# A spread order of the steps of a two-way recurrence, with products of ones where a step has no results or no modulation rows

## The reference

```python
def wkv_scan(state0, r, decay, kk, b, v, k, reverse):
    def step(S, inp):
        r_t, w_t, kk_t, b_t, v_t, k_t = inp
        sa = jnp.einsum("bhvk,bhk->bhv", S, kk_t)
        S = (S * w_t[:, :, None, :] - sa[..., None] * b_t[:, :, None, :]
             + v_t[..., None] * k_t[:, :, None, :])
        return S, jnp.einsum("bhvk,bhk->bhv", S, r_t)
...
        mod = jax.nn.silu(c) @ ada_w[l] + ada_b[l]
        sh1, sc1, g1, sh2, sc2, g2 = [m[:, None, :] for m in jnp.split(mod, 6, axis=-1)]
```

## Time and profile before

| | |
|---|---|
| median of 3 runs | 1587.11 us (1568.42 to 1589.66) |
| the profiled execution | 1576.66 us, span 1575.1 us |
| PE busy | 1493.3 us, 95% |
| DVE busy | 918.2 us, 58% |
| ACT busy | 598.1 us, 38% |
| mean granted clock of TensorE | 0.960 |
| mean DMA rate | 88 GB/s |

### The profile page before, as it was taken

One profiled execution on the slowest core, in us unless ns is written; L12 is line 12 of the kernel. 1 busy time (PEld: TensorE's weight loads), 2 busy tenths in 40 slices (PEclk: granted clock), 3 DMA queues, 4 the chain that ended last, 5 costly groups with the idle time before them and its releaser, 6 DMA issues.

```text
span 1575.1 us, 35522 instructions
## 1 busy us (share of the span) xinstructions
PE 1493.3 (95%) x14858; PEld 1232.4 (78%) x14858; DVE 918.2 (58%) x1499; ACT 598.1 (38%) x1037; POOL 271.8 (17%) x290
## 2 busy tenths in 40 slices
PE   5999989999999998999999998998999999999997
PEld 3788865788889777887877886877878888888885
DVE  4424245676668738888886224767565655555232
ACT  4422345333343534443443223536664322232221
POOL 0000024554443010111111121000021111111110
PEclk9999999778689999999999998999999999999998
DMA  9232201222220222232323222221112232232221
GB/s 370 97 110 79 81 0 56 76 91 84 83 63 4 83 81 80 80 107 80 107 82 108 92 92 81 88 81 55 54 54 82 106 107 85 101 107 92 92 92 72
DMA packets 38987, 139.15 MB, mean 88 GB/s; under 512 B 3152, under 2 KB 3664, under 8 KB 38480
## 3 DMA queue, kind: packets, MB, share of 16 engines
q1 hardware_dynamic: 38720, 135.24, 25.2%
q10 hardware_dynamic: 144, 2.10, 0.3%
HBM read 135.22 MB, written 2.10 MB: 87 GB/s over the span
## 4 chain that ended last, share of the span: by engine, by line
PE 80%; DVE 13%; ACT 3%; issue 3%; DMA 1%; ACTq 0%; DVEq 0%; SPq 0%
PE bank L716 56%; PE bank L898 9%; DVE ffn_sb L3153 5%; PE bank L725 3%; PE bank L662 2%; PE bank L992 1%; DVE w_up L2581 1%; PE bank L1064 1%; PE bank L1004 1%; PE bank L1554 1%; PE bank L929 1%; DMA arena<-w 1%; PE bank L655 1%; ACT w_up L1675 1%; ACT arena L2171 1%
## 5 line engine op out<-in xcount | busy, mean ns | idle before, releaser
L716 PE MATMUL bank<-hf_hi,w_up 128*128 128x512 f32 x1376 | 424.2, 389 | 0.0
L716 PEld LDWEIGHTS bank<-hf_hi,w_up 128*128 128x128 f32 x1376 | 258.4, 188 | 53.2
L716 PE MATMUL bank<-hf_lo,w_up 128*128 128x512 f32 x688 | 269.2, 391 | 4.5 <-DVE w_up L2581 4.5
L716 PE MATMUL bank<-act_hi,w_down 128*128 128x512 f32 x704 | 216.9, 389 | 0.0
L898 PEld LDWEIGHTS bank<-arena 64*64 64x64 f32 x4224 | 160.7, 154 | 35.7 <-issue 25.2
L898 PE MATMUL bank<-arena 64*64 64x32 f32 (+1 forms) x4224 | 172.3, 237 | 10.1 <-issue 6.1
L1675 ACT ACTIVATE w_up<-ring 128x1024 fp32r<-128x1024 f32 x87 | 91.9, 1058 | 215.7 <-PE bank L716 215.7
L2581 DVE TENSOR_TENSOR w_up<-ring,w_up 128x1024 fp32r<-128x1024 f32 x87 | 106.9, 1229 | 96.9 <-ACT w_up L1675 96.9
L716 PEld LDWEIGHTS bank<-hf_lo,w_up 128*128 128x128 f32 x688 | 129.2, 188 | 35.9 <-DVE w_up L2581 8.9
L3153 DVE SCALAR_TENSOR_TENSOR ffn_sb<-ffn_sb 128x512 f32<-128x512 f32 x176 | 151.5, 861 | 5.4
L716 PEld LDWEIGHTS bank<-act_hi,w_down 128*128 128x128 f32 x704 | 132.2, 188 | 27.4
(11 more groups left out here) (350 smaller groups left out, 2399.7 us busy)
## 6 DMA issues: line engine op xcount, KB each, us to landing
ring<-w SPq DMA_DIRECT2D x76, 1024.0 KB, 4.9
ring<-w SPq DMA_DIRECT2D x32, 704.0 KB, 4.0
ring<-w SPq DMA_DIRECT2D x64, 256.0 KB, 3.7
arena<-w SPq DMA_DIRECT2D x8, 1024.0 KB, 18.7
x<-xT SPq DMA_DIRECT2D x1, 2048.0 KB, 9.9
x<-xT ACTq DMA_DIRECT2D x1, 2048.0 KB, 8.4
outT<-x SPq DMA_DIRECT2D x4, 512.0 KB, 2.7
arena<-ctxT SPq DMA_DIRECT2D x1, 1024.0 KB, 18.9
```

Source lines behind the costliest of these rows:

```text
L716: ins = mm(out, w[:, a, k, :], of_block(b, k0 + k), start=first and k == 0 and m == 0, stop=last and k == n - 1 and m == 2)
```

## The change

The lists of PE, ACT and DVE are written in another order. On PE, in the second loop, both `state_terms` stand together behind level 3, `results` before and after nx of level 4, `turned` in level 5, the two `ada_part` in levels 5 and 6, and `scores` of the next chunk earlier. `ada_select(n)` and `mod_out(n)` of that loop move into the next step (as n - 1), and the wait of `scores` for `mod` is loosened by one for direction 1 where q > NCC. A new function `awake` issues one product of a 128x128 matrix of ones with itself, read four times over (512 columns), into bank[d][0], which nobody reads. It is called twice in a step without results (n = 2, 3) and twice in a step without modulation rows (n >= 7), 12 times in all. The matrix `warm` is made by one copy on ACT, and `rstd_c` is declared wider.

```diff
-        rstd_c = sb("rstd_c", [P, TC])
+        rstd_c = sb("rstd_c", [P, P])
+        warm = sb("warm", [P, P], F32R)[:, :]
...
                 if q > 0:
-                    pe.wait_ge(s[("ada_row", "mod")[d]], 8 + min(before, 8))
+                    rows = before - d if q > NCC else before
+                    pe.wait_ge(s[("ada_row", "mod")[d]], 8 + min(rows, 8))
...
+            warm_x = warm.unsqueeze(1).broadcast_to([P, 4, P])
+
+            def awake(n, d):
+
+                pe.wait_ge(s["low_tanh"], 2)
+                done("nk", d, 2 * min(n + 3, NC))
+                pe.wait_ge(s[("ada_row", "mod")[d]], 8 + min(n + 1, 8))
+                done("y_out", d, n - NCC + 1)
+                mm(bank[d][0][:, :], warm, warm_x, start=True, stop=True)
...
             for n in range(NCC - 2, NC - 1):
                 m, q = n + 1, n + 2
                 nx(m, 0, 2)
+                nx(m, 1, 2)
+                scores(q, 1)
                 updates(n, 0)
-                nx(m, 1, 2)
+                dx(m, 1, 2)
+                dx(m, 0, 2)
                 scores(q, 0)
...
                 results(n, 0)
+                if n < NCC:
+                    awake(n, 0)
                 nx(m, 0, 4)
...
+                ada_part(n, 0)
+                if n >= 7:
+                    awake(n, 0)
                 nx(m, 0, 6)
-                ada_select(n)
                 nx(m, 1, 6)
+                ada_part(n, 1)
+                if n >= 7:
+                    awake(n, 0)
                 dx(m, 0, 6)
                 dx(m, 1, 6)
...
             act_f(table_at, ones[:, 0:1], ACT.Exp)
+            act_f(warm, ones, ACT.Copy).then_inc(s["low_tanh"], 1)
```

192 lines of the change are left out of this document (96 added, 96 removed).

## The result

The changed kernel is slower, not faster: a median of 1604.86 us (4 runs, 1584.66 to 1605.89) against 1588.38 us (4 runs, 1568.42 to 1593.57), ratio 1.0161, 95% interval [1.0094, 1.0227]. The profiled execution took 1604.62 us, its span is 1602.9 us at a mean clock of 0.948 (before 1576.66, 1575.1 and 0.960). Ten later runs of the same kernel have a median of 1590.27 us and a ratio of 1.0086 [1.0024, 1.0149]; all 14 have a mean of 1594.6 us, against 1584.8 us over the 91 runs of the kernel before in this study. So the cost is about **10 us, 0.6%**, and the first four runs overstate it. Single runs of the kernel before lie between 1558.2 and 1607.5 us. The ratios leave out runs more than 1.5% above the fastest of their kernel, which here drops ordinary runs as well, so I give the mean of all runs with its standard error beside each ratio.

A forecast was written before the change was run, and what follows sets the result against it. PE's time was taken as the bound, with 87 us of the recurrence at half clock. 24.2 - 2.7 - 1.0 = 20.5 us gained from 1576.7 gives 1556, raised slightly to 1557 us; range 1538 to 1582.

The forecast's parts named there:

- What bounds the kernel: Whole kernel: PE's time counts nearly everywhere, TensorE busy 95%; in the recurrence 87 us run at half clock.
- what half clock costs: Recurrence steps: each microsecond at half clock costs 0.41 us, with 0.35 and 0.47 as ends.
- Step 1: PE's order in the second loop: heavy products spread among level groups cut half clock from 87 to 28 us, gaining 24.2 us.
- Step 4: Second loop: ada_select and mod_out one step later, DVE and ACT lists following PE's order; costed at nothing, DVE waits left to rivals.
- Rival D: Recurrence steps: PE's waits for DVE take the clock's place, 1 to 1.5 us a step; 1566 to 1575 us, chance 0.07.
- the prediction's own sign: Steps n = 4 to 6 in the later profile: clock 1.00 yet still over 23 us would mean Rival D.
- The rule that the prediction named: TensorE's clock is lost through PE's idle gaps between bursts of matmuls; the forecast held that step n = 8 disagrees.
- E: Recurrence up to n = 6: once lost, the clock does not come back, adding 65 us; 1642 us, chance 0.04.
- Step 2: Twelve products of ones in n = 2, 3 and 7 to 10: 0.222 us each, 2.7 us lost.
- Step 3: state_terms(n, 1) close behind updates(n, 1), waiting for ACT's copy: 1 us lost over nine steps, between 0 and 7.
- The base: Starting time: profiled run of 1576.7 us, median 10.4 us above it, difference supposed mostly half clock that the change takes away.

The follow-up runs named there:

- h4_masks_in_level5: The kernel before with only DVE's masks of the next scores (first_level) moved from level 4 to level 5; mean 1602.9 us, ratio 1.0142.
- h1_masks_and_turned: The changed kernel without the products of ones, with DVE's masks back in level 4 and PE's turned back in levels 3 and 4; mean 1604.5 us, ratio 1.014.
- i1_after_fill_ahead: The changed kernel with ten products of ones added in the step n = -1, behind its turned(m, 0); mean 1592.5 us.
- e8_after_again: The changed kernel run again with no edit; mean 1592.4 us, ratio 1.0086.
- e4_before_again: The kernel before run again with no edit; mean 1583.9 us, ratio 0.9893 against itself.

## Why the prediction was wrong

**What bounds the kernel, and what half clock costs: right.** Over the runs of each kernel the time grows by 0.35 to 0.48 us for each microsecond at half clock (0.45 over the 91 runs of the kernel before, 0.44 over all); 0.41 was taken.

**Step 1, the order on PE: this is the term that failed. 24.2 us of clock were forecast; over the whole kernel it gave none (139 us at half clock against 137).** What it said of n = 0 to 6 was right in kind and under half in size. Over the four profiles with the whole changed order these steps hold 47 us at half clock on average (41, 52, 37, 57), against 71 over five with the order before (86, 57, 83, 69, 62). The forecast took the 86 of one profile as the kernel's own and 28 for what remains. The gain is 24 x 0.43 = 10.3 us. Its direct cost was put at nothing, and there most goes back: PE stands 18.1 us instead of 13.2 in these steps, the four ones of n = 2, 3 cost about 1, and some 3 us are not accounted for. The steps together are 172.6 against 174.0 us, **1.4 us** gained, which profiles that spread over 9 and 13 us cannot tell from nothing. That n = 8 would keep its clock was wrong; it lost it in every profile of the changed order.

**Step 4, the DVE list "follows PE's order" and costs nothing: this is why step 1's gain did not stay.** It moved `first_level` beside POOL's burst and ahead of x_out. n = 7 and 8 take 48.8 us on average against 37.6, 11.2 us lost, of which (22 - 2) x 0.43 = 8.6 are clock and the rest ones and waits. In each of the eight steps n = 7 and 8 of these four profiles PE waits some 0.6 us for x_out and the clock falls less than 3 us later. Moving these two lines alone did the same in the kernel before. Putting them back alone did not cure the changed order, so there they are a cause and not shown to be the only one. 11.2 lost less 1.4 gained is 9.8 us, and the means of all runs differ by 1594.6 - 1584.8 = 9.8 too; that they meet is luck. The errors are 2 to 3 us on the means and more on the steps, and the sum leaves out what stands behind n = 8: from the start of n = 9 to the end the four profiles take 1084.6 us on average and the five 1081.4, with a fall of the clock for 10.2 us in n = 10 in three of the four, and for 3.4 us in two of the five. The account at equal clock is firmer: of the 8.9 us, some 3 are the ones, and PE stands 5.8 us longer from n = 0 to 8 (19.4 against 13.6).

**Rival D had the engine and not the price.** It said that DVE in line would take the clock's place at 1 to 1.5 us a step, as plain waits that only shrink the gain. The waits are small (0.6 us), but in n = 7 and 8 the clock fell behind each of them, and at 0.44 the 3.4 to 10.2 us at half clock that follow cost 1.5 to 4.5 us; and they fell on steps that had nothing to gain, which no rival looked at. By the prediction's own sign, n = 4 at full clock and 26.0 us speaks for D. Two readings behind D's low chance were off: PE waited for DVE's x_out too (1.2 us on L2769, beside the 1.6 on L2760), and DVE is busy 78% and not 81% in n = 8. The rule that the prediction named from the Trainium skill ("TensorE: Matmul & The Clock Gate", "HAM oscillation — how this bites in real kernels"), that the clock is lost through gaps, deserved more weight than I gave it by n = 8 alone: with PE's list untouched, small gaps ahead of a level run did decide. It is not the whole of it either: at the end of n = 6 the clock falls without a wait over 0.2 us in the first profile of before (449.5 us). E, the slower rival, was another mechanism and did not occur: the clock comes back in every step.

**Step 2, the ones:** forecast 2.7; 3.0 by their spacing, 2.0 in the changed order and 5.6 in the old one at equal clock. **Step 3, state_terms close behind updates:** no wait of PE for the update's copy appeared in its profiles, so its 1 us was nothing.

**The base.** The forecast was made against a profiled run of 1576.7 us and took the 10 us up to the median for more of the same half clock within the steps. Most of it was the stretch ahead of n = 0, which comes and goes without the change: filling it gave 10 us. The forecast and its range, 1538 to 1582, would have had to stand on the median, 1587; moved up by 10 us the range still ends below the 1594.6 of all 14 runs.

Left open: what sets off the "issue" stops beside the transfers, and why there is somewhat more of them; why one wait before a level run costs the clock and another does not; and a changed order whose masks keep clear of POOL in all steps, which was not found.

## What to carry to other kernels

Where TensorE's clock hangs on small products, look at every wait ahead of a run of them, also those of half a microsecond, and also in the steps that run well now: a list that is rewritten for all steps can lose there what it gains elsewhere. A moved item can cost by what runs beside it on another engine and by the item queued behind it; its engine's busy share does not tell. Before costing a change against one profile, take a second one of the same kernel: here one stretch that comes and goes was as large as the effect that was forecast. Where every run has its mean clock on record, take the time at equal clock beside the mean: here it told effects of 2 us apart where the means have errors of 3. And where a wait cannot be removed, useless products inside it cost little; at places where PE has no wait they cost what they give, or more.

## What was not expected of the hardware

- Waits of 0.55 to 1.09 us ahead of a run of 64x32 products were enough for a fall to 1.2 GHz where the same products without the waits kept the clock (`h4_masks_in_level5` against the kernel before). It is no fixed rule: a wait of 1.08 us in `h1_masks_and_turned` (476.4 us) and two of 0.60 and 0.61 in n = 10 of `i1_after_fill_ahead` (540.1 and 541.3 us) left it up.
- The time at half clock behind such a fall was anything from 3.4 us (469.8 to 473.2, `e8_after_again`) to 48 us (249.0 to 296.8, `e4_before_again`). In the longer one PE was busy 10.00 of 10 us, with 64x512 products among the small ones, and did not come back.
- The copies with a predicate took 440 ns alone and up to 927 ns beside POOL's products.
- Two executions of the same kernel differ in whether a stretch of 40 to 50 us at half clock is there: step n = 0 of the kernel before began at 278.1 us in one and at 301.8 in another.
